# Reordering the head, the attention start and the router tail of a two-layer hybrid block: order, banks and one tensor's place

## What is computed

```python
h = rmsnorm(x, norm1_g) * (1 + sc1) + sh1
u_a, q_b, k_b, v_b, q_c, kv_c, kr_c, gts = split_in(h @ w_in)
ya = pool_mixer(u_a, pool_w, pool_scale)                       # branch 0
yb = attention(qs, ks, vs, sink)                               # branch 1, 8 heads of 64
qm = rmsnorm(rmsnorm(q_c) @ w_q_b); km, vm = mla_kv(ckv, ...)  # branch 2, 8 heads of 96
yc = attention(qm, km, vm)
merged = sum(sigmoid(gts[i]) * (y[i] @ w_br[i]))               # i = 0, 1, 2
x = x + g1 * (merged @ w_out)
h = rmsnorm(x, norm2_g) * (1 + sc2) + sh2
aff = softmax(h @ w_router); vals, idx = top_k(aff, cap)       # each expert picks its tokens
x = x + g2 * scatter(vals * swiglu_expert(h[idx]))             # 16 experts, 1024 x 1024 x 3 each
```

## Time and profile before

| | us |
|---|---|
| median of 3 runs | 1815.55 (1815.0 to 1815.77) |
| the profiled execution: its time | 1816.19 |
| its span, first to last instruction | 1814.3 |
| PE busy | 1702.5 (94%) |
| DVE, ACT, POOL busy | 650.5, 288.4, 118.5 |

### The profile page before, as it was taken

How to read it: one execution, slowest core, us unless ns; L and a number is a source line. 1 busy time by engine, 2 the same in 40 slices (tenths; PEclk the granted TensorE clock), 3 DMA queues, 4 the chain that set the end, 5 groups by cost and what they waited for, 6 DMA issues and landing times.

```text
span 1814.3 us, 18937 instructions
## 1 busy us (share of the span) xinstructions
PE 1702.5 (94%) x7152; PEld 801.6 (44%) x7152; DVE 650.5 (36%) x1381; ACT 288.4 (16%) x733; POOL 118.5 (7%) x160
## 2 busy tenths in 40 slices
PE   6998999999999998898899989999999999988987
PEld 2455566654434333242245555666543433323322
DVE  1345655567212210221124466555661221211211
ACT  2233322111100010000022432221021000000000
POOL 1151000000000000000012500000000000000000
PEclk9999999999999999999999999999999999999999
DMA  9430333754899999999983213337648999999997
GB/s 383 178 122 24 116 116 116 278 200 182 356 429 432 431 430 432 430 431 429 429 359 119 99 47 116 116 128 294 234 189 359 429 430 431 431 431 431 430 431 315
DMA packets 49106, 533.81 MB, mean 294 GB/s; under 512 B 5840, under 2 KB 6896, under 8 KB 10384
## 3 DMA queue, kind: packets, MB, share of 16 engines
q1 hardware_dynamic: 45776, 524.39, 69.8%
q0 software_dynamic: 2112, 7.97, 1.2%
q10 hardware_dynamic: 1152, 0.56, 0.1%
HBM read 530.76 MB, written 2.13 MB: 294 GB/s over the span
## 4 chain that ended last, share of the span: by engine, by line
PE 72%; DMA 23%; DVE 3%; ACT 1%; issue 1%; SPq 0%; ACTq 0%; POOL 0%; DVEq 0%; POOLq 0%
PE bank L1957 21%; DMA ring<-in_w_moe 21%; PE bank L1583 12%; PE bank L1602 7%; PE bank L1648 6%; PE bank L1994 5%; PE bank L1819 5%; PE bank L1684 2%; DMA ring<-in_w_mix 2%; PE bank L1886 2%; PE bank L1745 2%; PE bank L1611 1%; PE bank L1720 1%; PE bank L1626 1%; PE bank L1571 1%; PE bank L1574 1%
## 5 line engine op out<-in xcount | busy, mean ns | idle before, releaser
L1583 PE MATMUL bank<-hT,ring 128*128 128x384 f32 x768 | 258.6, 490 | 0.0
L1957 PE MATMUL bank<-M,hT 128*64 128x512 f32 x1024 | 228.8, 595 | 21.0 <-DMA M<-in_w_moe 19.8
L1957 PE MATMUL bank<-ring,hT 128*64 128x512 f32 x1024 | 227.2, 595 | 11.4 <-DMA ring<-in_w_moe 11.4
L1583 PEld LDWEIGHTS bank<-hT,ring 128*128 128x128 f32 x768 | 143.4, 190 | 103.4 <-issue 7.8
L1957 PEld LDWEIGHTS bank<-M,hT 128*64 128x64 f32 x1024 | 72.5, 137 | 167.8 <-issue 136.8
L1957 PEld LDWEIGHTS bank<-ring,hT 128*64 128x64 f32 x1024 | 72.2, 137 | 158.2 <-issue 139.7
L1602 PE MATMUL bank<-M,ring 128*128 128x384 f32 x384 | 134.6, 494 | 5.6 <-ACT M L760 5.6
L1957 PE MATMUL bank<-ring,M 128*64 128x512 f32 x512 | 115.4, 596 | 18.7 <-DMA ring<-in_w_moe 18.7
L1957 PE MATMUL bank<-M 128*64 128x512 f32 x512 | 115.7, 595 | 12.3 <-DMA M<-in_w_moe 12.3
L1648 PE MATMUL bank<-ring,hT 128*128 128x512 f32 (+1 forms) x288 | 117.4, 567 | 2.8 <-DVE hT L1051 2.1
L951 ACT ACTIVATE hT<-bank 128x512 f32<-128x512 f32 x32 | 19.1, 598 | 571.6 <-PE bank L1957 571.6
(11 more groups left out here) (236 smaller groups left out, 1536.8 us busy)
## 6 DMA issues: line engine op xcount, KB each, us to landing
M<-in_w_moe SPq DMA_DIRECT2D x96, 2048.0 KB, 31.6
ring<-in_w_moe SPq DMA_DIRECT2D x96, 2048.0 KB, 30.6
ring<-in_w_mix SPq DMA_DIRECT2D x110, 1024.0 KB, 5.1
ring<-in_w_mix SPq DMA_DIRECT2D x4, 576.0 KB, 4.9
modrow<-in_bias_rows POOLq DMA_DIRECT2D x4, 512.0 KB, 5.7
g2slot<-in_bias_rows POOLq DMA_DIRECT2D x4, 512.0 KB, 7.3
M<-in_counts POOLq DMA_DIRECT2D x2, 768.0 KB, 12.4
out<-x SPq DMA_DIRECT2D x6, 256.0 KB, 2.0
```

Source lines behind the costliest of these rows:

```text
L1583: ins = mm(ps[:, 0:TOK], w[:, q, (j % 4) * P:(j % 4 + 1) * P], hT[:, 4 * h + q, :], start=(h == 0 and q == 0), stop=(h == 1 and q == 3))
L1957: ins = mm(bank[b][64 * e:64 * e + 64, :], lhs(e, 4 * h + q), w[:, q, :], start=(h == 0 and q == 0), stop=(h == 1 and q == 3))
```

## The change

Seven edits, all in order, banks and place; no arithmetic is added or removed.

1. `wq` runs tile by tile (both halves of tile 0 first) rather than half by half, on other banks, and each tile waits for its own copy.
2. ACT issues its four output DMAs behind the copies of `tkc`, `tkv` and `tq` rather than ahead of them.
3. The key transposes take other banks.
4. The first gate product stands between the second and the third key transpose; in step 0 PE goes branch, gate, probabilities, branch, probabilities. ACT and DVE follow: the tanh of the first gate ahead of the first exponentials, its merge ahead of the first `divide`.
5. The three `column` groups stand in steps 2, 4, 6.
6. In the tail `route(0)` stands ahead of the last `gate_row`, three of four sample gathers stand ahead of `turn_slots`, `turned(0, 0)` goes from DVE to ACT, and ACT's `router_part(0)` ahead of `normal_x(2)`.
7. `M` is declared behind `ring`. In the built program `ring` begins at byte 53,376 of a partition in both; `M` goes from 145,920 to 118,912.

```diff
@@ plan_banks
-            use(("wq", h, t), 1 + 3 * h + t)
+            use(("wq", h, t), 1 + 2 * t + h)
-            use(("tkm", t, h), ((3, 4), (5, 0), (7, 4), (1, 2))[t][h])
+            use(("tkm", t, h), ((7, 0), (3, 4), (3, 4), (5, 6))[t][h])
-        if m in (3, 5, 7):
-            use(("col", 6 + (m - 3) // 2), 5)
+        if m in (2, 4, 6):
+            use(("col", 5 + m // 2), 5)
@@ hybrid_step
         ring = sb("ring", [P, RING, UNIT])
+        M = sb("M", [P, 20160])
...
@@ ACT
-                for dst, src, s in ((outs[2][0, l], ktok[:, 0, :], ktok_ready), (outs[3][0, l], vtok[:, 0, :], None),
-                                    (outs[4][0, l], ckvtok[:, 0, :], ckvtok_ready), (outs[5][0, l], kr[:, 0, :], None)):
...
                 for t in range(T):
                     ps = wait_full(act, l, ("tkc", t))
...
                 for t in range(T):
                     ps = wait_full(act, l, ("tq", t))
                     read(l, ("tq", t), F(qT[:, :, t * P:(t + 1) * P], ps[:, :].rearrange("p (b t) -> p b t", t=P), ACT.Copy))
+
+                for dst, src, s in ((outs[2][0, l], ktok[:, 0, :], ktok_ready), (outs[3][0, l], vtok[:, 0, :], None),
+                                    (outs[4][0, l], ckvtok[:, 0, :], ckvtok_ready), (outs[5][0, l], kr[:, 0, :], None)):
...
+                gate_tanh(l, 0, 0)
                 for j in range(2):
                     exps(l, 0, j)
@@ ACT, tail
                 expert_exp(2)
+                turned(0, 0)
                 wait_full(act, l, ("wo", 1, 0))
                 normal_x(1)
                 square_x(0)
                 turned(0, 1)
+                router_part(0)
                 normal_x(2)
-                router_part(0)
                 expert_exp(0)
@@ DVE
                 for m in range(NM):
+                    if m == 0:
+                        merge(l, 0, 0)
                     for j in range(2):
                         divide(l, m, j)
-                    if m in (3, 5, 7):
-                        column(6 + (m - 3) // 2)
-                    merge(l, m // 4, 2 * m % 8)
+                    if m in (2, 4, 6):
+                        column(5 + m // 2)
+                    if m:
+                        merge(l, m // 4, 2 * m % 8)
...
@@ PE
                 for t in range(T):
                     wait_read(pe, l, ("tkc", t))
-                for h in range(2):
...
+                    for h in range(2):
+                        arrived(l, ("wq", h, 0))
...
-                for t in range(4):
+                for t in range(2):
+                    turn_heads("tkm", t, 3 + t)
+                gate(l, 0, 0)
+                for t in (2, 3):
                     turn_heads("tkm", t, 3 + t)
...
+                    if m == 0:
+                        branch(l, 0, 0)
+                        gate(l, 0, 1)
+                        turn_probs(l, 0, 0)
+                        branch(l, 0, 1)
+                        turn_probs(l, 0, 1)
+                        scores(l, 1)
+                        continue
                     gate(l, b, j)
-                    if m not in (0, 4):
+                    if m != 4:
                         values(l, m - 1)
@@ PE, tail
                 router(0)
+                route(0)
                 gate_row(11, 1)
-                route(0)
                 pe.wait_ge(xn2_ready, 3 * l + 2)
                 gather_sample(0, (0,))
                 turn_affinities(1, 0, 1)
-                gather_sample(0, (1,))
+                gather_sample(0, (1, 2))
                 turn_slots(1, 0, 1)
-                gather_sample(0, (2, 3))
+                gather_sample(0, (3,))
```

More of the change, by code:

```diff
@@ L296, in hybrid_step @@
         rinv = sb("rinv", [P, 2, 3])
-        M = sb("M", [P, 20160])
         def view(at, *dims):
@@ L803, in _ @@
                     read(l, ("u", g), F(upad[:, g, 152:408], ps[:, P:TOK], ACT.Copy))
-                for dst, src, s in ((outs[2][0, l], ktok[:, 0, :], ktok_ready), (outs[3][0, l], vtok[:, 0, :], None),
-                                    (outs[4][0, l], ckvtok[:, 0, :], ckvtok_ready), (outs[5][0, l], kr[:, 0, :], None)):
-                    if s is not None:
-                        act.wait_ge(s, 3 * l + 1)
-                    act.dma_start(dst, src).then_inc(cache_out, 16)
                 for t in range(T):
@@ L828, in _ @@
                     read(l, ("tq", t), F(qT[:, :, t * P:(t + 1) * P], ps[:, :].rearrange("p (b t) -> p b t", t=P), ACT.Copy))
+                for dst, src, s in ((outs[2][0, l], ktok[:, 0, :], ktok_ready), (outs[3][0, l], vtok[:, 0, :], None),
+                                    (outs[4][0, l], ckvtok[:, 0, :], ckvtok_ready), (outs[5][0, l], kr[:, 0, :], None)):
+                    if s is not None:
+                        act.wait_ge(s, 3 * l + 1)
+                    act.dma_start(dst, src).then_inc(cache_out, 16)
                 for t in range(T):
@@ L865, in _ @@
                     for j in range(2):
-                        gate_tanh(l, (2 * m + j) // 8, (2 * m + j) % 8)
+                        if m:
+                            gate_tanh(l, (2 * m + j) // 8, (2 * m + j) % 8)
+                        elif j == 0:
+                            gate_tanh(l, 0, 1)
                         if j == 0 and m not in (0, 4):
@@ L1311, in _ @@
                             sum_rows(6 + m // 2, m % 2, (0, 1))
-                    merge(l, m // 4, 2 * m % 8 + 1)
+                            if m == 0:
+                                merge(l, 0, 1)
+                    if m:
+                        merge(l, m // 4, 2 * m % 8 + 1)
                     if m + 1 < NM:
@@ L1429, in _ @@
                 number(P, TOK)
-                turned(0, 0)
                 add_mixed(1, 0)
@@ L1713, in _ @@
                     wait_read(pe, l, ("tkc", t))
-                for h in range(2):
-                    arrived(l, ("wq", h, 0))
-                    w = ring[:, slot_of(("wq", h, 0)), 0:3 * QR].rearrange("p (k n) -> p k n", n=QR)
-                    for t in range(T):
+                    for h in range(2):
+                        arrived(l, ("wq", h, 0))
+                        w = ring[:, slot_of(("wq", h, 0)), 0:3 * QR].rearrange("p (k n) -> p k n", n=QR)
                         ps = begin(l, ("wq", h, t))
```

## The result

| | before | after |
|---|---|---|
| median | 1815.55 | 1804.93 (5 runs, 1804.55 to 1808.51) |
| after / before | | 0.9948, interval 0.9933 to 0.9962 |
| the profiled execution | 1816.19 | 1807.8 |
| its span | 1814.3 | 1805.8 |
| start of the tq transposes, layer 0 | 112.81 | 114.88 |

The kernel is faster by 10.6 us. Forecast were 19.5 and 1796. The last two lines of the table name two places of the loss: the stretch that was reordered got 6.65 shorter in this execution rather than 9.7, and the expert half, in which no instruction moved, got 2.48 longer. A third stands in the row above them: the transposes start 2.07 later.

What follows compares the result with a forecast made beforehand. PE bounds layer 0 up to about 467 us, then DMA streaming expert weights. Savings of 1.58 + 1.43 + 3.62 + 0 + 3.1 = 9.7 per layer, twice 19.5, take 1816.19 to 1796.7; predicted 1796, range 1792 to 1805.

Steps and rivals of the forecast that it cites:

- the prediction's own signs of being wrong: Wait for query tile 2, PE waiting for DVE's keys, clock 0.50 in step 0, or a longer expert half.
- Direction and first half: Expert weight stream restarts when PE starts the experts, so each microsecond won before that shortens the layer; 9.7 per layer.
- Hidden anyway: Rival: the expert stream does not move with PE's start, so nothing arrives; 1815.5, chance 4%.
- Queries: Query products and first key/value products: two PE waits go, saving 1.58 and 1.43 us per layer.
- Keys, gate, step 0: Key transposes to step 1: old waits go, a new 2.7 us wait for DVE's merge comes; saves 3.62 per layer.
- E + 8.75: Start of the scores, counted from E, the start of the key transposes: 8.75 us later.
- S + 7.11: Second gate's start in step 0, counted from S, the start of the scores; forecast at S + 7.1.
- Columns: Column groups in steps 2, 4, 6: new wait of about 0.6 in step 2, net 0, between -0.8 and +0.8 per layer.
- Tail: Route to experts: route(0) 0.65 earlier, gathers 2.5 less if the clock stays up; saves 3.1 per layer.
- Edit 7: M's new place, half a 256-byte unit off: taken as 0, upper bound 38 us.
- M a little slower: Rival: each double transfer to M takes 0.07 us more, 6.5 us in all; 1802, chance 2%.
- The rival at 20%: PE's new 2.7 us idle in step 0 drops the clock once or twice; 1798 to 1799.5, chance 20%.

Runs made afterwards that it cites:

- a_mback: The changed kernel with M declared last again, all other edits kept; 1801.25 us, ratio 0.9919 to the kernel before.
- b_tail: The kernel before with the tail reorder (edit 6) alone; 1810.85 us, ratio 0.9974.
- b_mpad: The kernel before with 128 unused bytes ahead of M alone, M in its old place in the order; 1819.84 us (1 run).
- b_mfwd: The kernel before with M declared behind ring (edit 7) alone; 1820.08 us, ratio 1.0026.
- b_both: The kernel before with 128 unused bytes ahead of ring and of M, both on a 256-byte boundary; 1813.32 us, ratio 0.9990.
- b_keys: The kernel before with edits 3 and 4 alone (banks of the key transposes, first gate ahead); 1813.02 us, ratio 0.9977.
- best_al: The changed kernel with M last, early merge, columns in 3, 5, 7, ring and M on 256-byte boundaries; 1791.33 us, ratio 0.9866 to the kernel before.

## Why the prediction was wrong

The two steps that failed are the cost of edit 7, set to 0 and measured at 4.8 us, and the granted clock in the first half, taken to stay at 1.00 in the sum and worth up to 4.6. Both stand among the prediction's own signs of being wrong: the clock shows 0.50 in step 0, and the expert half is longer.

**Direction and first half: right.** That the stream moves with PE's start held in every kernel: with equal addresses the expert half kept its length (446.34 in before and in a_mback) while its start moved by 9.15. Hidden anyway is out, by that.

**Queries: right.** 3.19 against 3.0, and ACT's four DMAs hurt nobody. **Keys, gate, step 0: right in its order**, E + 8.75 and S + 7.11 being what the working gave. From E to the gate of step 1 a_mback takes 27.12 (145.62 to 172.74), with 27.15 worked out. One reading there was off by 0.1 without effect: by the earlier trace rows the second head's maxima end at 162.55, not near 162.45. **Columns: right at full clock**, wait of 0.67 and a net of nothing. **Tail: 2.8 against 3.1**, since route(0) still waits 0.49 for ACT and came 0.5 earlier rather than 0.65 (455.49 in b_tail against 455.87, again from tq on), with the clock at 1.00 as assumed. The prediction took the low clock of the old tail as given; b_mpad shows it absent in both layers, so this part of the gain, some 1.4 a layer, depends on the execution of the kernel before. The sum of all is 9.8 a layer against 9.7 (344.30 of 354.11).

**Edit 7: wrong, the first step that failed.** It was costed at 0, because the ring, off the boundary, was no slower than M, on it. This compares the two destinations inside one kernel, where they share a stream in which the price, if one is paid, falls on both: in the changed kernel ring and M take 4.895 alike, too. The earlier trace rows could show what one tensor off does, and that is next to nothing. It couldn't show what two do. The right reading was: no row of this trace has both off, so the cost is unknown, and its lower end is not its value. What it cost is 0.66% on all doubles, 5.0 us between the profiled executions and 4.8 in b_mfwd. Against the edit stood the Trainium skill (DMA: Bandwidth & Descriptors, How a descriptor splits into AXI transactions): a descriptor that does not start on 256 B is charged for the bytes between the boundary below and its start. The estimate of 0.8% on the moved half, 3.7 us, which the prediction worked out from that table, came near to the cost. The rule so read still does not give the runs: by it the ring would pay in the kernel before already, an estimate of 1.9 us a layer from the same 0.8%, and with both tensors on the boundary (b_both) a layer is only 0.66 faster. The 2% for "M a little slower" were far too low for a cost that no row excluded.

**The clock: the second step that failed. The rival at 20% came true, and at one place more.** The wait of 2.54 was named with its risk; its drops cost 1.6 by the medians. The column step was costed by PE's waits alone. There a wait of 0.67 is followed by sixteen one-column records, and behind them stand two of the three drops of the changed kernel's profiled execution; by the medians they cost some 3 us over both layers, the larger part, of which the start of the kernel may hold some. Whether the wait or the small records bring the drop is not separated. The argument against, that the work around is dense, was the wrong one to trust: the second gate runs in dense work, and its clock fell.

Together: 1796.7, 4.8 for edit 7 and up to 4.6 for the clock give up to 1806.1. Measured are 1804.93, at the very end of the range; that it still lies inside is luck, since the range was drawn for the clock and the columns and not for edit 7. The mean granted clock was 0.998 in the three fastest executions and 0.995 and 0.996 in the other two.

## What to carry over

A change of allocation is a change of addresses. Compare each large DMA destination before and after, all of them together, and try a pad of a few bytes before you argue from an equal rate. Where a wait of some 2.5 us, or a short wait followed by one-column matmuls, is put on a PE that is the bound, count the clock as well, as an expected loss that differs between executions, and look for another order of the engine that is waited for: here one merge moved up took 1.9 of the 2.54 us away and, with the columns put back, most of the spread.

## What the runs showed of the hardware

- The stream pays in full for unaligned SBUF destinations only where both buffers in rotation are off 256 bytes: 4.895 against 4.863 us per 2 MB, in rows of 16 KB. With one of them off, two doubles of eight take 4.875 to 4.884, where the stream goes from the one that is off to the other; with none off, none does. Why is open; the runs show only that it isn't the place of M, and that M 64 or 128 bytes off is the same.
- The granted clock differs between executions of one kernel with the same waits: 1.00 throughout in one of a_mback's five, 0.997 in the other four. The spread of the times is widest in b_keys, which has the new wait and the old tail (8.9 us, ten runs), and least in best_al, which has neither (0.7 us, four runs).
- The same piece of program can get more or less of the low clock without a change in it: in the tail, which b_keys and b_mpad leave as it was, 460 to 466 us ran at 0.50 throughout in b_keys and at 0.72 in the mean in the kernel before, and in b_mpad 455 to 467 us ran at 1.00.
